# The fifth key tile of each attention block in split form

## Chip, cores and metric

The kernel runs on one core of a Trainium2 chip. The metric is the time of one execution on the device in microseconds (us). Engines are named as TensorE (PE in the profile, its weight loads PEld), VectorE (DVE), ScalarE (ACT), GpSimd (POOL) and SyncE (SP).

## The reference

A trunk of two layers over 1024 latent tokens and 256 context tokens, width 1024. The first layer (gMLP and S5 mixers) is not touched by the change. The second is grouped-query attention: 8 query heads of 128, 2 key/value heads, so 4 query heads share one key/value head. Queries and keys are normalised and rotated, and every latent query sees all 1280 keys:

```python
def _attend(q, k, v):
    s = jnp.einsum('btkgd,bskd->bkgts', q, k).astype(jnp.float32) * (HEAD_DIM ** -0.5)
    p = jax.nn.softmax(s, axis=-1).astype(v.dtype)
    return jnp.einsum('bkgts,bskd->btkgd', p, v)

# in _odd_layer, per block of 128 queries:
    o = lax.map(lambda qi: _attend(qi, k_all, v), qb)
    x = x + gt * ((o_lat * jax.nn.silu(gate[:, n_ctx:])) @ w_out)
```

All values are float32. A final RMSNorm follows.

## The kernel before

The attention stage is a loop over 16 blocks `i` (8 groups of 128 queries x 2 key/value heads). A block holds 4 heads x 128 queries = 512 columns. Its 1280 keys are `TT` = 10 tiles `t` of 128. All engines run over the same running number `m = 10 i + t`, each with its own program, and semaphores tie them together.

**Split form.** A float32 product is made of rounded high parts and low parts (the rest after rounding, in the fp32r type): high x high, high x low and low x high, three matmuls. For the values this is `Vh`/`Vl` and `p_hi`/`p_lo`. Tiles listed in `plain` are multiplied natively instead: one float32 instruction on `Vt` and `PF`, which the trace shows as two MATMUL records.

**Per tile.** TensorE makes the scores (`scores`, lines 2189 to 2191, for t < 2 with one more matmul that subtracts the row maximum, line 2186). ScalarE takes the exp into `PF[m % 5]` (line 1101) and, unless the tile is plain, rounds it into `p_hi` (line 1104, recorded as line 737). The low part `p_lo = PF - p_hi` is made on GpSimd for the tiles in `on_pool` (1 and 6, line 714) and on VectorE for the other split tiles (line 1681), one step of the loop later. GpSimd also adds up `PF` over the tiles in `psum_p` (line 710). TensorE multiplies with the values (`values`) four tiles later (`LAG` = 4): line 2206 for plain tiles, lines 2208 to 2210 for split ones. `PF[4]` and `PF[3]` lie in `region_b`, the others in `region_c`.

**Per block, besides.** TensorE makes the maxima's scores of the next block (`max_scores`, line 2161) at t = 0, 2, 4, 6, one head each; VectorE reduces them (`row_max`, line 1627) at the same t; at t = 8 TensorE transposes the four maxima (`max_rows`) and VectorE turns them into `neg_max` (line 1633), which the first scores of the next block read. The sums of the block before come by `row_sums` on TensorE at t = 4 (line 2219), `sums_copy` on ScalarE, `sums_to_tokens` on TensorE at t = 5, the reciprocal on VectorE (`sums_inverse`, t = 5, line 1647), four transposes `over_sums` on TensorE at t = 6 (recorded as line 1742), and `gate_over_sums` and `output` on VectorE at t = 7. Rounding of the next queries and their low part (`q_rest`, line 1622) come at t = 9.

**Order.** Each engine works in program order. TensorE at a step t of block i: `values(m - 4)`, `scores(i, t)`, then `row_sums`, `sums_to_tokens` or `over_sums` (t = 4, 5, 6), then `max_scores` or `max_rows`. VectorE at a step: `p_lo` of the tile before, then `row_max`, then `sums_inverse`, `gate_over_sums` and `output`, `neg_max` or `q_rest`. These two lines of `values` and VectorE's loop are the ones on which the change acts:

```python
                if t in plain:
                    mm = te.matmul(o, Vt[:, t, hd], PF[m % NP], start=t == 0, stop=t == TT - 1)
...
                if m and (m - 1) % TT not in on_pool + plain:
                    dve.wait_ge(*p_done(m - 1))
```

**V's split.** At the start of the loop ScalarE and VectorE split V in four pieces, per key/value head and half. `split_tiles(half)` gives the tiles of a half that are not plain: 0 to 3 and 5 to 8.

Of the kernel before, what the change touches and what calls it, by code (L numbers as in the profile page):

```python
# [61 lines left out]
def build(nc, x, ctx_in, xt_in, cols_in, w_mod, we_in, we_out, gm_w_s, gm_b_s,  # L62
          lam_in, s5_log_dt, b_in, c_in, s5_d, s5_w_glu, wo_in, wo_out, q_norm_g, k_norm_g, final_g,
          ident_in, cos_in, sin_in, out):
    with ExitStack() as es:
# [311 lines left out]
        def x1_done(t):  # L377
            return s_o_ok, TT + t + 1

        plain, on_pool = (4, 9), (1, 6)  # L380

        def upto(tiles, m):
            return len(tiles) * (m // TT) + sum(t <= m % TT for t in tiles)
# [1984 lines left out]
```

## Time and profile before

| | us |
|---|---|
| median of 3 runs | 1199.05 (1198.66 to 1199.93) |
| the profiled execution | 1199.77 |
| its span on the core | 1198.0 |
| TensorE busy | 1150.5 (96%) |
| VectorE busy | 826.9 (69%) |
| ScalarE busy | 501.8 (42%) |
| GpSimd busy | 427.4 (36%) |

The attention loop runs from about 801 to about 1107 us. In a timeline row the first number is the start in us from the span's beginning, the second the duration; then engine, line, operation, output and inputs, shapes and count. A number in brackets at the end is the idle time of the engine ahead of that instruction and who ended it. Records of one engine can overlap by some hundredths, since an instruction starts while the one before is still writing.

### The profile page before, as it was taken

The page shows a single profiled execution, that of the slowest core. Times are in us where ns is not written, and L with a number is a line of the kernel's source. Part 1 is how long each engine was busy: PE and PEld are TensorE (multiplying, and loading weights), DVE is VectorE, ACT ScalarE, POOL GpSimd, SP SyncE. Part 2 cuts the span into 40 slices and gives each one's busy share as a digit, 9 for nine tenths or more (in the row PEclk, how much of TensorE's full clock was granted, in tenths as well). Part 3 has the DMA queues.
Part 4 walks back from the last instruction along what each step waited for, and adds up shares of the span by engine and source line. Part 5 has one row for each costly group of instructions (what it writes and reads, how often), then busy time and mean ns, then how long its engine had stood idle before and what let it go on. Part 6 is the DMA issues. An engine that isn't in the chain of part 4 may idle for free.

```text
span 1198.0 us, 16737 instructions
## 1 busy us (share of the span) xinstructions
PE 1150.5 (96%) x6498; PEld 943.5 (79%) x6498; DVE 826.9 (69%) x1264; ACT 501.8 (42%) x948; POOL 427.4 (36%) x336
## 2 busy tenths in 40 slices
PE   2899999999999999999999999999999999999996
PEld 2678889887888987878888888876777777777885
DVE  5599959899916365037839968249888888884237
ACT  3444567110014642134523442246666666664022
POOL 4810100000000002542211112248898888897232
PEclk9899999999999999999999999999999999999999
DMA  9933896435421946213121122230000000000403
GB/s 339 369 115 114 197 283 221 142 112 176 156 90 55 323 148 233 71 41 134 38 71 36 36 80 79 88 124 9 10 18 10 18 19 10 18 10 27 165 21 130
DMA packets 81023, 129.83 MB, mean 108 GB/s; under 512 B 12944, under 2 KB 43024, under 8 KB 80144
## 3 DMA queue, kind: packets, MB, share of 16 engines
q1 hardware_dynamic: 71120, 113.96, 28.2%
q10 hardware_dynamic: 9824, 14.80, 3.5%
q8 instruction: 52, 0.85, 0.3%
q14 instruction: 27, 0.22, 0.1%
HBM read 97.81 MB, written 30.93 MB: 107 GB/s over the span
## 4 chain that ended last, share of the span: by engine, by line
PE 88%; DVE 6%; DMA 3%; ACT 1%; issue 1%; POOL 1%; SPq 0%; DVEq 0%; ACTq 0%
PE ps L1877 10%; PE ps L1879 10%; PE ps L1878 10%; PE ps L1888 6%; PE ps L1889 6%; PE ps L1890 6%; PE ps L2161 3%; PE ps L1742 3%; DMA weight_ring<-in_w_mod 3%; PE ps L2191 3%; PE ps L2190 3%; PE ps L2189 3%; PE ps L2245 2%; PE ps L2247 2%; PE ps L2246 2%; PE ps L2208 2%
## 5 line engine op out<-in xcount | busy, mean ns | idle before, releaser
L1877 PE MATMUL ps<-w_hi,a_hi 128*128 128x512 f32 x448 | 177.6, 397 | 4.7 <-DVE b_lo L1221 3.3
L1878 PE MATMUL ps<-w_lo,a_hi 128*128 128x512 f32 x448 | 175.4, 392 | 0.0
L688 POOL TENSOR_TENSOR region_b<-region_b,region_d 128x512 f32<-128x512 f32 x20 | 26.3, 1328 | 397.0 <-DVE region_d L1533 397.0
L1879 PE MATMUL ps<-w_hi,c_lo 128*128 128x512 f32 x368 | 143.3, 389 | 0.0
L1888 PE MATMUL ps<-a_hi,w_hi 128*128 128x512 f32 (+1 forms) x384 | 137.9, 359 | 0.0
L1889 PE MATMUL ps<-b_lo,w_hi 128*128 128x512 f32 (+1 forms) x384 | 136.0, 354 | 0.0
L1890 PE MATMUL ps<-a_hi,w_lo 128*128 128x512 f32 (+1 forms) x384 | 135.9, 354 | 0.0
L681 POOL TENSOR_TENSOR w_lo<-weight_ring,w_hi 128x2048 fp32r<-128x2048 f32 x14 | 65.1, 4652 | 185.5 <-ACT w_hi L737 185.5
L1627 DVE TENSOR_REDUCE small<-ps 128x1 f32<-128x1280 f32 x64 | 95.2, 1487 | 41.7 <-PE ps L2161 41.4
L710 POOL TENSOR_TENSOR region_c<-region_c 128x512 f32<-128x512 f32 x80 | 108.5, 1356 | 26.2 <-ACT region_c L1101 25.1
L1877 PEld LDWEIGHTS ps<-w_hi,a_hi 128*128 128x128 f32 x448 | 84.8, 189 | 24.4 <-issue 5.1
L710 POOL TENSOR_TENSOR region_c<-region_c,region_b 128x512 f32<-128x512 f32 x64 | 98.7, 1542 | 9.2
L1878 PEld LDWEIGHTS ps<-w_lo,a_hi 128*128 128x128 f32 x448 | 84.9, 189 | 17.2
L1101 ACT ACTIVATE region_c<-ps 128x512 f32<-128x512 f32 x96 | 57.3, 597 | 77.2 <-PE ps L2191 74.6
L1681 DVE TENSOR_TENSOR p_lo<-region_c,p_hi 128x512 fp32r<-128x512 f32 x64 | 81.5, 1273 | 11.7 <-ACT p_hi L737 11.7
L737 ACT ACTIVATE w_hi<-weight_ring 128x2048 fp32r<-128x2048 f32 x29 | 55.6, 1916 | 71.3 <-DMA weight_ring<-in_we_out 30.3
L1888 PEld LDWEIGHTS ps<-a_hi,w_hi 128*128 128x128 f32 x384 | 72.5, 189 | 11.4 <-issue 1.1
L1890 PEld LDWEIGHTS ps<-a_hi,w_lo 128*128 128x128 f32 x384 | 72.5, 189 | 10.2
L1879 PEld LDWEIGHTS ps<-w_hi,c_lo 128*128 128x128 f32 x368 | 69.1, 188 | 14.4
L1889 PEld LDWEIGHTS ps<-b_lo,w_hi 128*128 128x128 f32 x384 | 72.6, 189 | 9.6
L737 ACT ACTIVATE region_d<-ps 128x512 f32<-128x512 f32 (+5 forms) x90 | 49.1, 605 | 34.8 <-DMA bop_scratch<-region_d 13.9
L2189 PE MATMUL ps<-q_t_hi,kd_hi 128*128 128x512 f32 x128 | 62.9, 492 | 0.7 <-ACT region_c L1101 0.5
(253 smaller groups left out, 2679.1 us busy)
## 6 DMA issues: line engine op xcount, KB each, us to landing
weight_ring<-in_w_mod SPq DMA_DIRECT2D x10, 2048.0 KB, 9.1
weight_ring<-in_we_in SPq DMA_DIRECT2D x10, 1024.0 KB, 6.8
weight_ring<-in_wo_in SPq DMA_DIRECT2D x10, 1024.0 KB, 5.1
weight_ring<-cop_t_scratch SPq DMA_DIRECT2D x4, 1536.0 KB, 7.7
region_c<-in_w_mod SPq DMA_DIRECT2D x2, 2048.0 KB, 20.0
bop_scratch<-region_d ACTq DMA_DIRECT2D x16, 256.0 KB, 2.9
cop_t_scratch<-region_d SPq DMA_DIRECT2D x8, 512.0 KB, 7.2
weight_ring<-bop_scratch SPq DMA_DIRECT2D x2, 2048.0 KB, 11.3
```

The costliest lines, as they stand in the source:

```text
L681: g.tensor_tensor(wl, slot_raw(u), wh.bitcast(F32), ALU.subtract).then_inc(s_w_lo, 1)
L710: g.tensor_tensor(psum_p[:, i % 2], PF[(m - 1) % NP] if t == 1 else psum_p[:, i % 2], PF[m % NP], ALU.add).then_inc(s_a_sum, 1)
L737: return a.activation(o, i, ACT.Copy)
L1627: v.tensor_reduce(smax[:, i % 2, h:h + 1], ps[:, 0:3, :].rearrange("p b n -> p (b n)")[:, 0:TOK], AX.X, ALU.max).then_inc(s_a_max, 1)
L1681: v.tensor_tensor(p_lo[:, (m - 1) % NP], PF[(m - 1) % NP], p_hi[:, (m - 1) % NP].bitcast(F32), ALU.subtract).then_inc(s_a_pld, 1)
L1877: te.matmul(o, th, wh[:, k % 4], start=k == 0, stop=False)
L1878: te.matmul(o, th, wl[:, k % 4], start=False, stop=False)
L1879: last = te.matmul(o, tl, wh[:, k % 4], start=False, stop=k == KT - 1)
L1888: te.matmul(o, wh[:, k, fs], th, start=k == 0, stop=False)
L1889: te.matmul(o, wh[:, k, fs], tl, start=False, stop=False)
L1890: last = te.matmul(o, wl[:, k, fs], th, start=False, stop=k == KT - 1)
L2189: te.matmul(o, kh, qh, start=False, stop=False, skip_group_check=t >= 2)
```

## The change

Tile 4 leaves the list of plain tiles; tile 9 stays in it.

```diff
-        plain, on_pool = (4, 9), (1, 6)
+        plain, on_pool = (9,), (1, 6)
```

What follows from it in each of the 16 blocks: TensorE multiplies tile 4 with three split matmuls (lines 2208 to 2210) instead of the native one (line 2206), and waits ahead of them for its low part instead of for its exp; ScalarE rounds tile 4 into `p_hi` after its exp; VectorE makes `p_lo` of tile 4 at step t = 5, behind the row maximum of t = 4 and ahead of `sums_inverse`. ScalarE's exp of tile 9 also waits for the rounding and the low part of tile 4, whose buffer it takes. `split_tiles(0)` becomes 0 to 4, so that the two pieces of V of the first half grow from 512 to 640 columns on ScalarE and on VectorE; the counts of `p_done`, `p_rest_done` follow. GpSimd's work is the same.

## Rows read from the trace of the kernel before

**Rows 1.** Table by stretches: one block; busy per engine, granted clock, DMA share, GB/s
```profile
951.10:969.67 18.57, 18.57 (x92) 14.17 (x90) 15.93 (x16) 12.10 (x22) 16.29 (x12) 1.00 0.04 15
```

**Rows 2.** Timeline of TensorE: the slots of tile 3 and tile 4
```profile
945.51 0.39 PE L2208 MATMUL ps<-p_hi,v_hi 128*128 128x512 f32 x1
...
946.67 0.40 PE L2191 MATMUL ps<-q_t_hi,k_t_lo 128*128 128x512 f32 x1
946.90 1.02 PE L2206 MATMUL ps<-region_b 128*128 128x512 f32 x2
...
948.23 0.40 PE L2191 MATMUL ps<-q_t_hi,k_t_lo 128*128 128x512 f32 x1
```

**Rows 3.** Timeline of VectorE, the next block
```profile
954.19 0.68 DVE L1681 TENSOR_TENSOR p_lo<-region_c,p_hi 128x512 fp32r<-128x512 f32 x1
...
961.01 1.48 DVE L1627 TENSOR_REDUCE small<-ps 128x1 f32<-128x1280 f32 x1
962.41 0.17 DVE L1647 RECIPROCAL small<-ps 128x4 f32<-128x4 f32 x1
963.05 1.21 DVE L1681 TENSOR_TENSOR p_lo<-region_c,p_hi 128x512 fp32r<-128x512 f32 x1 [0.47 <-ACT p_hi L737]
...
968.38 0.67 DVE L1633 SCALAR_TENSOR_TENSOR neg_max<-ps,ident 4x512 fp32r<-4x512 f32 x1
```

**Rows 4.** Timeline of ScalarE, the same block
```profile
959.73 0.27 ACT L737 ACTIVATE mod_row<-ps 128x128 f32<-128x128 f32 x1
...
962.38 0.63 ACT L737 ACTIVATE p_hi<-region_c 128x512 fp32r<-128x512 f32 x1
```

**Rows 5.** Timeline of TensorE, the same block: around `over_sums`, and its end
```profile
962.83 0.59 PEld L1742 LDWEIGHTS ps<-ident,small 128*128 128x128 f32 x4
963.07 0.60 PE L1742 MATMUL ps<-ident,small 128*128 128x128 f32 x4
963.42 0.83 PE L2161 MATMUL ps<-k_t_hi,q_t_hi 128*128 128x512 f32 x3
...
969.67 0.39 PE L2186 MATMUL ps<-neg_max,ones_r 128*128 128x512 f32 x1
```

**Rows 6.** Timeline of GpSimd: the sum of tile 5 in the same block
```profile
962.43 1.28 POOL L710 TENSOR_TENSOR region_c<-region_c 128x512 f32<-128x512 f32 x1 [0.20 <-ACT region_c L1101]
```

**Rows 7.** Timeline of VectorE and GpSimd at two near ties ahead of the loop
```profile
590.88 0.43 DVE L1133 TENSOR_TENSOR region_b<-region_b,rec_tmp 128x256 f32<-128x256 f32 x1
590.91 4.86 POOL L681 TENSOR_TENSOR w_lo<-weight_ring,w_hi 128x2048 fp32r<-128x2048 f32 x1 [19.41 <-ACT w_hi L737]
...
664.62 4.61 POOL L681 TENSOR_TENSOR w_lo<-weight_ring,w_hi 128x2048 fp32r<-128x2048 f32 x1 [14.11 <-ACT w_hi L737]
664.65 4.86 DVE L1133 TENSOR_TENSOR region_d<-region_d 128x256 f32<-128x256 f32 x1
```

**Rows 8.** Timeline of VectorE and TensorE behind the loop: a reciprocal that is waited for
```profile
1111.77 0.18 DVE L1647 RECIPROCAL small<-ps 128x4 f32<-128x4 f32 x1 [14.64 <-PE ps L1742]
1112.01 0.65 PE L1742 MATMUL ps<-ident,small 128*128 128x128 f32 x4 [0.28 <-DVE small L1647]
1112.42 0.48 PE L1877 MATMUL ps<-w_hi,ot_hi_a 128*128 128x512 f32 x1
```

**Rows 9.** Timeline of block 0: GpSimd, VectorE and TensorE
```profile
813.45 1.29 POOL L710 TENSOR_TENSOR region_c<-region_c 128x512 f32<-128x512 f32 x1
813.51 1.78 DVE L1681 TENSOR_TENSOR p_lo<-region_c,p_hi 128x512 fp32r<-128x512 f32 x1
...
820.62 0.47 PE L2186 MATMUL ps<-neg_max,ones_r 128*128 128x512 f32 x1 [0.54 <-issue]
```

**Rows 10.** Timeline of block 1: GpSimd (two records in one row), VectorE and TensorE
```profile
832.48 2.99 POOL L710 TENSOR_TENSOR region_c<-region_c 128x512 f32<-128x512 f32 x2
832.51 0.17 DVE L1647 RECIPROCAL small<-ps 128x4 f32<-128x4 f32 x1
833.03 0.60 PE L1742 MATMUL ps<-ident,small 128*128 128x128 f32 x4
```

## The prediction

> **What bounds the kernel now.** I read the table by stretches first, for one attention block out of the middle of the loop [rows 1]: in 18.57 us TensorE is busy for all 18.57, at a granted clock of 1.00 (its 2.4 GHz level), VectorE for 15.93, GpSimd for 16.29 and ScalarE for 12.10. There are 16 such blocks. So a block lasts as long as its TensorE instructions, and whatever makes TensorE wait is lost. VectorE has 2.6 us of air in a block, but where the air lies decides. The timeline by engine shows that: VectorE has no idle time (a number in brackets) ahead of the third row maximum and of the reciprocal behind it, and 0.47 us after that [rows 3]. The reciprocal is what TensorE needs next.
>
> **TensorE, the gain.** With tile 4 out of `plain`, its two native records become three split matmuls. In the slot of tile 4 the native form takes from 946.90 to the last score matmul at 948.23, 1.33 us; the same slot of tile 3 in split form from 945.51 to 946.67, 1.16 us [rows 2]. Both hold two of the three score matmuls besides, so the difference is the edit's: 0.17 us a block. The slot lies in blocks 0 to 15, but in block 0 TensorE waits for VectorE anyway, so 15 x 0.17 = 2.6 us is the most that the change can give. The Trainium skill (FP8 and Floating Point Precision, section TensorE Precision Notes) says that true FP32 takes four passes through the array. By that rule three passes save a quarter, and where the rows give 0.17 us the page would give somewhat more, about 0.2 us; the sum below would fall by some 0.6 us, and its sign would stay.
>
> **ScalarE, nothing.** It gets one rounding copy a block, `p_hi` of tile 4, 0.63 us like that of tile 5 [rows 4]. Behind it is queued the copy of the sums, which runs from 959.73 to 960.00 and would end by 960.67. TensorE fetches the sums one tile ahead of the transposes of 963.07 [rows 5]: less 1.16 us for the tile and 0.35 us for itself that is 961.56, so 0.9 us of cover are left. If it were gone, each 0.1 us would be 0.1 us on TensorE.
>
> **VectorE, the price.** It gets one subtraction a block, `p_lo` of tile 4, and the loop puts it at t = 5 ahead of `sums_inverse`. The queue there is: row maximum at 961.01, reciprocal at 962.41 to 962.58, idle 0.47, `p_lo` of tile 5 at 963.05 [rows 3]. Its data are ready by about 960.5, so it would start where the reciprocal starts today. Queued behind it are the reciprocal and, for that, TensorE's four transposes of `over_sums`, whose weight load begins at 962.83 and whose first matmul at 963.07, with the row-max matmuls of the next head at 963.42 [rows 5]. The idle 0.47 us comes after the reciprocal and so is no cover for it; the cover is 0.25 us, from 962.58 to 962.83.
>
> How long the subtraction takes depends on GpSimd. With GpSimd idle it took 0.68 us (954.19), and 1.21 and 1.78 us when GpSimd ran a tensor operation [rows 3, 9]. The rows show how: `p_lo` at 963.05 ends at 964.26, 0.55 us after GpSimd's operation of 962.43 ends at 963.71 [rows 3, 6]; that of 813.51 ends at 815.29, 0.55 us after the operation of 813.45 ends at 814.74 [rows 9]. So with two inputs from SBUF the one that comes second waits until the other is through. At the place of the new subtraction both come together: VectorE would start at 962.41, GpSimd's sum of tile 5 at 962.43 [rows 3, 6]. Near ties elsewhere tell who goes first [rows 7]: at 590.88 VectorE starts 0.03 us ahead, keeps its 0.43 us, and GpSimd's operation is stretched to 4.86 from the 4.61 us of its twin at 664.62; at 664.65, 0.03 us behind GpSimd, VectorE is held for 4.86 us. Here VectorE is ahead by 0.02 us and goes first, I estimate. Both ends: 0.61 us to the next start (0.68 less the 0.07 by which these records overlap) if it wins, 1.77 us if it loses (962.43 + 1.28 + 0.55, less the overlap, against 962.41). I take 0.61, the nearest rows in distance.
>
> Then the reciprocal starts at 963.02 and ends at 963.19. In the last block TensorE really waits for one: it ends at 1111.95, the transposes start 0.06 us later and the next matmul 0.41 us after that [rows 8], against 0.35 us when nothing waits [rows 5]. So the row-max matmul comes at 963.19 + 0.06 + 0.41 = 963.66 and not 963.42: a loss of 0.24 us, less 0.17 gained, net +0.07 us.
>
> Is another wait then last? GpSimd is pushed back by 0.53 us in its sum of tile 5, `p_lo` of tile 5 now waits for it and ends near 964.79, the fourth row maximum starts at 964.71 and `neg_max` at about 968.90 instead of 968.38 [rows 3]. It ends at 969.57; TensorE needs it for the first matmul of the next block at 969.67 today, 969.74 then [rows 5]. It fits, by about 0.1 us. Bounds for a steady block: -0.05 (half the loss) to +0.30 us (that margin gone too).
>
> **Block 0.** Here VectorE is late and TensorE waits for it, at the end of the block 0.54 us for `neg_max`, until 820.62 [rows 9]. All added here is paid in full. At its place (813.51) GpSimd starts 0.06 us ahead, so the subtraction takes what `p_lo` of tile 5 takes there now, 1.78 us, 1.71 from start to start. `split_tiles(0)` now spans five tiles, so two ScalarE copies and two VectorE subtractions of V have 640 instead of 512 columns: 0.13 us more each on VectorE (1280 columns took 1.40 us from start to start, 512 take 0.61 [rows 3]), two of them before `neg_max`. Together 1.71 + 0.26 = 1.97 us; bounds 0.9 and 2.3.
>
> **Block 1.** GpSimd's start is 0.03 us ahead of VectorE's reciprocal at 832.51 [rows 10], so the subtraction waits: 832.48 + 1.28 (GpSimd's 962.43 row) + 0.55 gives 834.31, reciprocal to 834.41, transposes at 834.47 against 833.03 [rows 10]. 1.44 + 0.06 - 0.17 = +1.33 us; bounds 0 and 1.4.
>
> **Last block.** No row maxima are there; the new subtraction ends close to the reciprocal's old place: about 0.1 us lost, 0.17 gained, -0.1 us. Behind the loop nothing changes.
>
> **Sum.** 1.97 + 1.33 + 13 x 0.07 - 0.1 = +4.1 us. The profiled execution took 1199.77 us, 1198.0 of it the span; it would be 1203.9. It lies 0.7 us above the median of 1199.05, so the median becomes 1203.1. With the bounds: 0.9 + 0 - 0.7 - 0.1 = +0.1 to 2.3 + 1.4 + 3.9 - 0.1 = +7.5 us.
>
> **Rivals.** (1) GpSimd wins the tie in every block. Then the subtraction ends at 964.26, the reciprocal at 964.35, the row-max matmul comes at 964.82: 1.40 lost, 0.17 gained, 13 x 1.23 = 16.0, total +19.2 us, 1218.2 us. It decides from a GpSimd start 0.01 to 0.03 us earlier against VectorE. For it speaks that the distance is tiny and that a subtraction behind a row maximum lost at 0.06 us [rows 9]; against it stand the near ties [rows 7]. The Trainium skill (GPSIMD Engine Reference, section Key points) says that GpSimd shares its SBUF interfaces with VectorE and contends with instructions of two SBUF inputs; by that rule alone this case is the plain one, and the trace agrees that they contend, though not that VectorE always pays. (2) Faster: TensorE does not wait at `over_sums`, since the reciprocal is out by 962.77 after all. The deciding point is 0.4 us: VectorE would have to reach this place by that much earlier. Then 15 x 0.17 = 2.6 us come off, 1196.5 us if block 0 costs nothing. Against it: no idle VectorE time ahead of the third maximum and the reciprocal [rows 3]. (3) The steady blocks come out even and block 0 or 1 absorbs part: +0.5 to +2 us, about 1200.5. For it: the bounds of the small terms.
>
> **How the numbers follow.** Forecast 0.72 (its own spread 1200.5 to 1206.6, since the small terms will hardly all lie at the same end), rival 1 with mixtures 0.12, rival 2 0.06, rival 3 0.10. The range 1199.6 to 1207.5 leaves out rival 1 and rival 2 and a little of rival 3. A measurement of this kernel tells 0.2%, 2.4 us, from no change. Faster by that needs rival 2 nearly whole: 0.05. Within it: rival 3, the low end of the forecast (below 1201.4) and the rest of rival 2: 0.18. Slower: 0.77.
>
> **What would show it.** Steady blocks of about 18.64 us; the reciprocal 0.6 us later behind the third row maximum, with `p_lo` of tile 4 of 0.68 us between; GpSimd's sum of tile 5 stretched to about 1.8 us; TensorE idle some 0.2 us before the transposes of `over_sums`. If that subtraction reads 1.8 us, rival 1 holds; if TensorE has no idle time there, rival 2. Wrong also if `neg_max` ends last at a block's border, or if block 0 grows by less than 1 us.

## The result, and the profile after

| us | before | after |
|---|---|---|
| median of 6 runs of each | 1198.88 (1197.69 to 1199.93) | 1203.43 (1202.88 to 1203.74) |
| the profiled execution | 1199.77 | 1203.29 |
| its span | 1198.0 | 1201.5 |

The ratio of after to before is 1.0033, interval 1.0024 to 1.0043: slower, by 4.6 us in the medians and by 3.5 us in the two profiled spans. The forecast was 1203.1, made of +4.1 us on the span and the place of the profiled execution of before among its runs. On the span +4.1 is 0.6 us too high; that the median comes within 0.3 us is in part chance.

The attention loop was measured block by block, from the first row-max matmul of a block (line 2186) to that of the next:

| block | before | after | difference | forecast |
|---|---|---|---|---|
| 0 | 19.82 | 21.80 | +1.98 | +1.97 |
| 1 | 19.02 | 18.72 | -0.30 | +1.33 |
| 2 | 18.59 | 18.66 | +0.07 | +0.07 |
| 3 to 13, each | 18.573 | 18.683 (18.65 to 18.72) | +0.110 | +0.07 |
| 14 | 18.14 | 18.64 | +0.50 | +0.07 |
| last, and all behind it | 117.29 | 117.29 | -0.01 | -0.1 |

With the stretch ahead of the loop (+0.07) that is 1.98 - 0.30 + 0.07 + 11 x 0.110 + 0.50 - 0.01 + 0.07 = +3.5 us. The forecast was near because its errors cancel: one term, block 1, is 1.6 us too high, and the others are 1.0 us too low together. That is luck.

The first line of the page of after (busy time, share, instructions) answers to the table of before: VectorE has 18.6 us more, about 13 of it the 16 new subtractions (14 of 0.68 us; those of block 0 and the last block are held by GpSimd and take 1.78) and the rest mostly other operations held longer behind GpSimd; ScalarE has 10 us more; TensorE is as long as it was, 1150.8 us against 1150.5, since records last longer while they wait: in the middle block below they cover 18.70 of 18.71 us.

```profile
PE 1150.8 (96%) x6514; PEld 943.4 (79%) x6514; DVE 845.5 (70%) x1280; ACT 512.1 (43%) x964; POOL 435.6 (36%) x336
```

The table by stretches of after, block 0 and a block out of the middle (length; busy time of TensorE, its weight loads, VectorE, ScalarE, GpSimd; granted clock; DMA share, GB/s), answers to [rows 1]:

```profile
800.87:822.67 21.80, 16.84 (x71) 11.83 (x70) 19.55 (x15) 15.75 (x26) 17.15 (x12) 1.00 0.26 85
953.45:972.16 18.71, 18.70 (x93) 14.21 (x92) 17.08 (x17) 12.73 (x23) 16.86 (x13) 1.00 0.06 16
```

In block 0 TensorE stands still for 5 us, VectorE for 2.3. In the middle block TensorE seems never to stand still. That is a trap: a matmul's record lasts some 0.4 us, while the next one starts 0.23 us after it when nothing waits. A wait under 0.17 us hides inside a record, and only the distance from start to start shows it.

The timeline of VectorE in that block of after, from the third row maximum to `neg_max`, answers to [rows 3]:

```profile
963.46 1.48 DVE L1627 TENSOR_REDUCE small<-ps 128x1 f32<-128x1280 f32 x1
964.86 0.68 DVE L1681 TENSOR_TENSOR p_lo<-region_b,p_hi 128x512 fp32r<-128x512 f32 x1
965.45 0.17 DVE L1647 RECIPROCAL small<-ps 128x4 f32<-128x4 f32 x1
965.55 1.67 DVE L1681 TENSOR_TENSOR p_lo<-region_c,p_hi 128x512 fp32r<-128x512 f32 x1
...
969.92 1.53 DVE L1681 TENSOR_TENSOR p_lo<-region_c,p_hi 128x512 fp32r<-128x512 f32 x1
971.38 0.67 DVE L1633 SCALAR_TENSOR_TENSOR neg_max<-ps,ident 4x512 fp32r<-4x512 f32 x1
```

The timeline of GpSimd, same stretch, answers to [rows 6]:

```profile
964.88 1.79 POOL L710 TENSOR_TENSOR region_c<-region_c 128x512 f32<-128x512 f32 x1 [0.20 <-ACT region_c L1101]
967.10 1.29 POOL L710 TENSOR_TENSOR region_c<-region_c 128x512 f32<-128x512 f32 x1 [0.43 <-POOL region_c L710]
968.35 1.30 POOL L714 TENSOR_TENSOR p_lo<-region_c,p_hi 128x512 fp32r<-128x512 f32 x1
969.60 1.30 POOL L710 TENSOR_TENSOR region_c<-region_c 128x512 f32<-128x512 f32 x1
```

VectorE starts the new subtraction at 964.86, GpSimd its sum of tile 5 at 964.88. VectorE goes first and takes 0.68 us; GpSimd waits inside its record, 1.79 instead of 1.28 us. It is so in blocks 1 and 3 to 14; in block 2 GpSimd starts 0.25 us behind, and the order is the same. And the timeline of TensorE, at `over_sums` and at the block's end, answers to [rows 5]:

```profile
965.27 0.40 PE L2191 MATMUL ps<-q_t_hi,k_t_lo 128*128 128x512 f32 x1
965.68 0.65 PE L1742 MATMUL ps<-ident,small 128*128 128x128 f32 x4
966.09 0.71 PE L2161 MATMUL ps<-k_t_hi,q_t_hi 128*128 128x512 f32 x2
...
971.92 0.40 PE L2210 MATMUL ps<-p_hi,v_lo 128*128 128x512 f32 x1
972.16 0.46 PE L2186 MATMUL ps<-neg_max,ones_r 128*128 128x512 f32 x1
972.46 0.40 PE L2189 MATMUL ps<-q_t_hi,k_t_hi 128*128 128x512 f32 x1
```

The transposes come 0.06 us after the reciprocal's end (965.62), 0.41 instead of 0.23 us behind the matmul before, and the next matmul 0.41 instead of 0.35 us behind them: 0.24 us, as forecast. But the border costs too. `neg_max` ends at 972.05, its matmul starts 0.11 us later, and the one behind that 0.30 instead of 0.23 us later, because its weights weren't loaded ahead: another 0.07 us. (At 8 of the 15 borders the matmul starts 0.101 to 0.102 us after `neg_max`, the least in this run, so it waits itself.) TensorE's weight load for the matmul at this border, in after and then in before, where it begins 0.24 us ahead of its matmul of 969.67 and not 0.04 us:

```profile
972.12 0.19 PEld L2186 LDWEIGHTS ps<-neg_max,ones_r 128*128 128x128 f32 x1 [0.23 <-issue]
...
969.43 0.19 PEld L2186 LDWEIGHTS ps<-neg_max,ones_r 128*128 128x128 f32 x1
```

The waits of TensorE's weight loads, from 820 to 1080 us of after (total, times, longest), show the two places (for the second the profile names no engine; experiment 5 shows that it is `neg_max`); in before the first is missing and the second has one wait:

```profile
PEld ps L1742 <- DVE small L1647: 6.2, 14, 0.4
...
PEld ps L2186 <- issue: 4.5, 14, 1.5
```

### The profile page after: what moved, and what is told of

It reads as the page before. It is cut to its first block, busy times and chain, and to the rows that moved or that the text cites. A ratio compares the mean times of both kernels' runs of the same rounds, so it can differ in the third digit from the quotient of the medians.

```text
span 1201.5 us, 16817 instructions
## 1 busy us (share of the span) xinstructions
PE 1150.8 (96%) x6514; PEld 943.4 (79%) x6514; DVE 845.5 (70%) x1280; ACT 512.1 (43%) x964; POOL 435.6 (36%) x336
## 4 chain that ended last, share of the span: by engine, by line
PE 86%; DVE 6%; DMA 3%; POOL 2%; issue 1%; ACT 1%; SPq 0%; POOLq 0%; DVEq 0%; ACTq 0%
PE ps L1877 10%; PE ps L1879 10%; PE ps L1878 10%; PE ps L1888 6%; PE ps L1890 6%; PE ps L1889 6%; PE ps L1742 3%; PE ps L2161 3%; DMA weight_ring<-in_w_mod 3%; PE ps L2189 3%; PE ps L2190 3%; PE ps L2191 3%; PE ps L2208 2%; PE ps L2210 2%; PE ps L2247 2%; PE ps L2246 2%
## 5 line engine op out<-in xcount | busy, mean ns | idle before, releaser
L710 POOL TENSOR_TENSOR region_c<-region_c 128x512 f32<-128x512 f32 x80 | 116.0, 1450 | 21.9 <-ACT region_c L1101 19.0
L1681 DVE TENSOR_TENSOR p_lo<-region_c,p_hi 128x512 fp32r<-128x512 f32 x64 | 90.4, 1412 | 4.0 <-ACT p_hi L737 4.0
L2191 PE MATMUL ps<-q_t_hi,k_t_lo 128*128 128x512 f32 x160 | 62.7, 392 | 0.0
```

The lines of the kernel that those rows point to most:

```text
L710: g.tensor_tensor(psum_p[:, i % 2], PF[(m - 1) % NP] if t == 1 else psum_p[:, i % 2], PF[m % NP], ALU.add).then_inc(s_a_sum, 1)
L1681: v.tensor_tensor(p_lo[:, (m - 1) % NP], PF[(m - 1) % NP], p_hi[:, (m - 1) % NP].bitcast(F32), ALU.subtract).then_inc(s_a_pld, 1)
L2191: te.matmul(o, kl, qh, start=False, stop=True, skip_group_check=t >= 2).then_inc(s_a_s, 1)
```

## The experiments

Unless said otherwise, the edit is made to the changed kernel. "Steady" is the length of blocks 3 to 13. Times are medians; the kernel before was measured again beside the experiments, and its medians there, 1199.7 to 1200.0, lie about 1 us above the one of the table. So an experiment is compared with after by blocks or by the profiled spans, 1201.5 us for after and 1198.0 for before.

**1. Without the subtraction.** Tile 4 is multiplied in three parts, but its high part stands in for the low one. The counts of `p_rest_done` follow.

```diff
-                if m and (m - 1) % TT not in on_pool + plain:
+                if m and (m - 1) % TT not in on_pool + plain + (4,):
...
-                    te.matmul(o, Vh[:, t, hd], p_lo[:, m % NP], start=False, stop=False)
+                    te.matmul(o, Vh[:, t, hd], p_hi[:, m % NP] if t == 4 else p_lo[:, m % NP], start=False, stop=False)
```

> The changed kernel without VectorE's subtraction for tile 4. What is left out: the low part of tile 4's exp; TensorE multiplies p_hi of tile 4 twice instead of p_hi and p_lo. ScalarE's rounding and the larger V pieces stay. Theory: the price is VectorE's subtraction alone. Then a steady block, border to border, is 18.57 - 0.17 = 18.40 us, block 0 is 19.82 + 0.26 = 20.1 us, and the span is 2.0 to 2.5 us below that of the kernel before. Rival (the split matmuls or ScalarE's copy cost as much as they bring): a steady block stays at 18.57 to 18.68 us and the span is not below the kernel before.

1196.45 us against 1199.96 (ratio 0.9972, interval 0.9961 to 0.9983). Steady 18.380, block 0 20.14. So TensorE gains 18.573 - 18.380 = 0.193 us a block by the split form, and the rest of after is VectorE's subtraction: 18.683 - 18.380 = 0.303 us a steady block, 1.66 us in block 0. The remaining 0.3 us of block 0 is put down to V's wider pieces, which this kernel keeps; no run took them away alone. The profiled span is 1195.4 us, 2.6 below before (expected 2.0 to 2.5); the 3.5 us in the medians are more than the blocks account for.

**2. The reciprocal first.** If the reciprocal is what TensorE lacks, it could go ahead of the new subtraction.

```diff
+                if i and t == 5:
+                    sums_inverse(i - 1)
                 if m and (m - 1) % TT not in on_pool + plain:
...
-                if i and t == 5:
-                    sums_inverse(i - 1)
```

> The changed kernel with one order turned round: VectorE computes the reciprocal of the sums first and subtracts tile 4 behind it. Theory (the share of SBUF with GpSimd decides): the subtraction then starts about 0.1 us later, 0.08 us behind GpSimd's sum of tile 5 and no longer 0.02 us ahead of it, and is held for about 1.75 us; the wait at over_sums is gone, but row maximum and neg_max come 1 to 1.5 us later and end last at the block's border: a steady block of 19.5 to 20.0 us, the span 12 to 20 us above the changed kernel. Rival (only the place of the reciprocal in VectorE's order costs): the wait at over_sums is gone and nothing takes its place, a steady block of 18.40 to 18.50 us, the span 2.5 to 3.5 us below the changed kernel.

1220.10 us (ratio 1.0169, interval 1.0153 to 1.0186), steady 20.03. The transposes no longer wait, and the span is 16 us longer than that of after (1217.5 against 1201.5). VectorE's timeline, then GpSimd's:

```profile
971.51 0.17 DVE L1647 RECIPROCAL small<-ps 128x4 f32<-128x4 f32 x1
971.60 1.75 DVE L1683 TENSOR_TENSOR p_lo<-region_b,p_hi 128x512 fp32r<-128x512 f32 x1
973.27 1.79 DVE L1683 TENSOR_TENSOR p_lo<-region_c,p_hi 128x512 fp32r<-128x512 f32 x1
...
971.51 1.28 POOL L710 TENSOR_TENSOR region_c<-region_c 128x512 f32<-128x512 f32 x1 [0.18 <-ACT region_c L1101]
```

The reciprocal's 0.09 us are enough for GpSimd to be first. (In block 2, where GpSimd comes later, VectorE stays first and the block takes 18.77 us.) The subtraction is held until 0.55 us after GpSimd's sum, and the next one behind another operation of GpSimd. TensorE pays later, for a row maximum and for `neg_max`:

```profile
976.52 0.27 PE L1742 MATMUL ps<-ident,small 128*4 128x128 f32 x1 [0.43 <-DVE small L1627]
...
980.14 0.47 PE L2186 MATMUL ps<-neg_max,ones_r 128*128 128x512 f32 x1 [0.82 <-issue]
```

**3. Losing the tie.** A copy of one column goes ahead of the subtraction on VectorE, nothing else.

```diff
+                if m % TT == 5:
+                    v.tensor_copy(small[:, 334:335], small[:, 0:1])
```

> The changed kernel with one tiny VectorE copy of one column (about 0.07 us from start to start) ahead of the subtraction of tile 4 in each block. Theory: it turns the near tie round, GpSimd goes first, the subtraction reads about 1.75 instead of 0.68 us, the reciprocal comes 1.1 to 1.2 us later, and a steady block grows from 18.68 to 19.8 us: 15 to 17 us in all for 16 tiny instructions. Rival (the subtraction's length has nothing to do with who starts first): the block grows by the 0.07 us of the copy, 1 us in all.

1216.48 us in one run, steady 19.76 to 19.82. VectorE, GpSimd and TensorE:

```profile
970.85 0.14 DVE L1680 COPY small<-small 128x1 f32<-128x1 f32 x1
970.91 1.78 DVE L1683 TENSOR_TENSOR p_lo<-region_b,p_hi 128x512 fp32r<-128x512 f32 x1
972.62 0.17 DVE L1647 RECIPROCAL small<-ps 128x4 f32<-128x4 f32 x1
...
970.87 1.28 POOL L710 TENSOR_TENSOR region_c<-region_c 128x512 f32<-128x512 f32 x1 [0.20 <-ACT region_c L1101]
...
972.84 0.65 PE L1744 MATMUL ps<-ident,small 128*128 128x128 f32 x4 [1.18 <-DVE small L1647]
```

The copy moves the subtraction by 0.06 us, from 0.02 us ahead of GpSimd to 0.04 behind. That costs 1.1 us a block, and TensorE's wait is now plain to see. Block 2 is the check within the run: GpSimd starts a quarter of a microsecond later there, VectorE stays first in spite of the copy, and the block takes 18.65 us.

**4. The subtraction on GpSimd.** GpSimd has the lowest share of busy time on the page, 36%.

```diff
-        plain, on_pool = (9,), (1, 6)
+        plain, on_pool = (9,), (1, 4, 6)
```

> The changed kernel with the subtraction of tile 4 on GpSimd (on_pool = (1, 4, 6)). Theory: VectorE's queue ahead of the reciprocal is as in the kernel before, GpSimd has 2.3 us of air in a block and takes 1.28 more, so a steady block is 18.40 us, block 0 within 0.5 us of the kernel before, and the span 1.5 to 2.5 us below the kernel before. Rival (GpSimd becomes the bound, or holds VectorE longer): GpSimd's air is not where it is needed, row_sums or neg_max wait for it, a steady block of 18.6 us or more.

1216.42 us (ratio 1.0136, interval 1.0120 to 1.0151), steady 19.65. My theory missed by 1.2 us a block. The 36% are an average over the whole span; inside the loop GpSimd has no such room. The table by stretches, 40 us of the loop, and TensorE waiting for it:

```profile
960.00:1000.00 40.00, 38.45 (x187) 29.16 (x186) 34.43 (x31) 25.78 (x45) 38.42 (x28) 1.00 0.05 14
...
976.79 0.50 PE L2208 MATMUL ps<-p_hi,v_hi 128*128 128x512 f32 x1 [0.77 <-POOL p_lo L714]
```

GpSimd is busy for 38.42 of 40 us and is now what the block lasts on: its operations take 1.72 to 1.75 us where VectorE's turn comes first.

**5. `neg_max` earlier.** In the last step of a block `neg_max` goes ahead of VectorE's subtraction of tile 7 (the step's `p_lo`), which is held by GpSimd.

```diff
+                if i + 1 < 2 * LT and t == 8:
+                    neg_max(i + 1)
                 if m and (m - 1) % TT not in on_pool + plain:
...
-                if i + 1 < 2 * LT and t == 8:
-                    neg_max(i + 1)
```

> The changed kernel with neg_max ahead of the subtraction of tile 7 on VectorE (t = 8), all else as it is. Theory: of a steady block's 18.68 us, about 0.06 us are TensorE's wait for neg_max at the border and the rest of the loss against 18.38 us is the wait at over_sums. neg_max then starts 1.4 us earlier, the border wait goes, the wait at over_sums stays: a steady block of 18.62 us, the block ahead of the last 18.2 instead of 18.64 us; blocks 0 and 1 together 0.5 to 1 us shorter, the span 1.5 to 2.5 us below the changed kernel. Rival (the border wait costs nothing, the loss of 0.30 us is all at over_sums): steady blocks stay at 18.68 us.

1200.03 us against 1199.73 of before (ratio 1.0006, interval 0.9997 to 1.0015). Blocks 3 to 13 are 18.61, block 14 is 18.16, blocks 0 and 1 together 0.99 us shorter than in after, the span 2.7 us shorter. So the border's wait was real, and it was nearly all that block 14 had lost. The wait for the reciprocal stays: 18.61 - 18.38 = 0.23 us.

**6. Block 0 as before.** Tile 4 stays native in block 0 alone. V's tile 4 is then split by itself, later in block 1.

```diff
+        def is_plain(m):
+            return m % TT in plain or m == 4
...
+                if m == 16:
+                    dve.wait_ge(s_v_hi, 5)
+                    dve.wait_ge(s_a_pv, 1)
+                    v.tensor_tensor(Vl[:, 4], Vt[:, 4], Vh[:, 4].bitcast(F32), ALU.subtract).then_inc(s_v_lo, 1)
```

> The changed kernel with tile 4 native in block 0 alone; V's tile 4 is split by itself in block 1. Theory: block 0 falls from 21.80 to 19.8 us as in the kernel before. Block 1 then begins as in the kernel before, where GpSimd's sum started 0.03 us ahead of VectorE, so the subtraction of tile 4 is held there, as the prediction had it: block 1 of 20.2 to 20.5 us, the span 0.2 to 0.6 us below the changed kernel. Rival (VectorE is first in block 1 in any case): block 1 of 18.7 to 19.1 us, the span about 2 us below the changed kernel.

1204.09 us in one run: block 0 is 19.83 again, and block 1 becomes 21.31, where 20.2 to 20.5 were expected. Nothing is saved: the span is 0.8 us above that of after. This is the experiment on the forecast's block 1, which was worked out as if block 0 ended as before; here it does. VectorE, GpSimd and TensorE in block 1:

```profile
832.86 1.79 DVE L1689 TENSOR_TENSOR p_lo<-region_b,p_hi 128x512 fp32r<-128x512 f32 x1
...
832.83 1.28 POOL L716 TENSOR_TENSOR region_c<-region_c 128x512 f32<-128x512 f32 x1
...
834.80 0.65 PE L1754 MATMUL ps<-ident,small 128*128 128x128 f32 x4 [1.25 <-DVE small L1655]
...
838.22 0.47 PE L2222 MATMUL ps<-p_hi,v_hi 128*128 128x512 f32 x1 [0.78 <-DVE v_lo L1700]
```

GpSimd is 0.03 us ahead and the subtraction takes 1.79 us, as forecast. V's extra piece, which this edit brings in and the expectation had at nothing, costs more than the idle 0.78 us: the matmul of 838.22 starts 1.18 us behind the one of 837.04 instead of 0.23, and the next one 0.30 us behind it instead of 0.23, 1.02 us in all. The other wait, at `over_sums`, counts in the same way (1.65 instead of 0.24 us ahead of the transposes and 0.41 instead of 0.35 behind them, less the gain of 0.19) for +1.28 us. The two add up to the 2.3 us by which block 1 is longer than before, and +1.33 was forecast for the second.

**7. GpSimd told to wait.** Experiment 2, with the sum of tile 5 on GpSimd held until the subtraction of tile 4 is done.

```diff
+                    if t == 5:
+                        pool.wait_ge(*p_rest_done(m - 1))
```

> The changed kernel with the reciprocal first on VectorE, as in b_recip_first, and GpSimd's sum of tile 5 waiting until the subtraction of tile 4 is done. Theory: the order costs nothing once the turn on SBUF is fixed; the subtraction reads 0.68 us, neither over_sums nor neg_max is waited for, a steady block of 18.38 us as without the subtraction; block 0 of 20.7 to 21.3 us since it stays VectorE's; the span 1.0 to 2.0 us below the kernel before. Rival (GpSimd's chain of sums or VectorE's queue is late by the wait): a steady block of 18.5 us or more.

1204.41 us (ratio 1.0039, interval 1.0025 to 1.0052), where 1.0 to 2.0 us below before were expected: the rival held. Block 0 is 20.00, better than expected, since VectorE now goes first there too. Blocks 1 and 2 are 18.42 and 18.50, then it gives way to 18.82 to 19.15. GpSimd held for the subtraction and TensorE waiting for GpSimd, in block 8; then VectorE's subtraction ahead of `neg_max` and TensorE at the border, in block 5:

```profile
965.19 1.63 POOL L712 TENSOR_TENSOR region_c<-region_c 128x512 f32<-128x512 f32 x1 [0.68 <-DVE p_lo L1685]
...
970.29 0.50 PE L2210 MATMUL ps<-p_hi,v_hi 128*128 128x512 f32 x1 [0.41 <-POOL p_lo L716]
...
911.87 1.70 DVE L1685 TENSOR_TENSOR p_lo<-region_c,p_hi 128x512 fp32r<-128x512 f32 x1
...
914.27 0.47 PE L2188 MATMUL ps<-neg_max,ones_r 128*128 128x512 f32 x1 [0.20 <-issue]
```

The order costs GpSimd 0.68 us of idle time a block. Its later operations come later, the subtraction of tile 7 is held behind one of them for 1.70 us, and `neg_max` starts 17.22, 17.73 and 18.07 us after the border in blocks 1, 2 and 3. From block 2 on TensorE waits for it at the end of every block but block 8. There VectorE comes first instead (0.72 us), and TensorE waits for the low part that GpSimd makes; at 19.15 us it is the longest of these blocks.

**8. Experiments 6 and 7 together.**

> g_pool_after and f_block0_native together. Theory: block 0 as in the kernel before (19.8 us), steady blocks 18.38 us, the span 2.3 to 3.0 us below the kernel before, a ratio of 0.9975 to 0.998. Rival: what block 0 saves comes back in block 1 (over 19.4 us), and the span is no lower than that of g_pool_after.

1204.79 us (ratio 1.0042, interval 1.0030 to 1.0055). The rival held again: block 0 is 19.84, but block 1 is 20.37, with the wait for V's extra piece. Blocks 2 and 3 are 18.40 and 18.38, then 18.71, 18.83 and on as in 7, so the waits at the border begin in block 4 instead of block 2.

**9. The transposes later.** On TensorE, `over_sums` goes behind the row-max matmuls of the same step.

```diff
-                if i and t == 6:
-                    over_sums(i - 1)
                 if i + 1 < 2 * LT:
...
+                if i and t == 6:
+                    over_sums(i - 1)
```

> The changed kernel with TensorE's four transposes over_sums behind the row-max matmuls of t = 6 instead of ahead of them, 0.57 us later. Theory: the wait at over_sums goes, since the reciprocal is done by then, but neg_max ends when it did, so TensorE only meets it earlier at the block's border: a steady block of 18.60 to 18.66 us with 0.2 to 0.3 us of waiting at neg_max, the span 0.3 to 1.0 us below the changed kernel. Rival (the wait at over_sums is the whole loss): a steady block of 18.38 to 18.42 us, the span some 3.5 us below the changed kernel.

1203.50 us against 1199.95 (ratio 1.0027, interval 1.0018 to 1.0037), steady 18.70, neither the 18.60 to 18.66 of the theory nor the rival's 18.38. The waits of TensorE's weight loads from 820 to 1080 us show the other one alone, and grown:

```profile
PEld ps L2186 <- issue: 8.1, 14, 1.6
```

The wait for the reciprocal is gone, and nothing is won: `neg_max` by itself costs 0.32 us a block. The near tie is as near as the trace can show here: in block 5 both engines start at 906.97, VectorE 0.003 us ahead, and VectorE takes 0.68 us, GpSimd 1.82.

**10. Both orders together (5 and 9).**

> The changed kernel with both orders changed: over_sums behind the row-max matmuls of t = 6, and neg_max ahead of the subtraction of tile 7. Theory: both waits for VectorE go, the near tie stays won, and a steady block is that without the subtraction, 18.38 to 18.42 us; the span 1.5 to 2.5 us below the kernel before, a ratio of 0.9980 to 0.9990. Rival (a third wait takes their place, in VectorE's or GpSimd's queue): a steady block of 18.5 us or more and a span not below the kernel before.

1198.86 us against 1199.95 (ratio 0.9989, interval 0.9980 to 0.9998): 1.1 us under before (1.5 to 2.5 expected) and, by the spans, 4.4 us under after. The 1.1 us are a difference whose interval ends just short of 1 and that is smaller than what this kernel's measurement can tell from no change. Blocks 4 to 13 take 18.353 each, block 14 17.91. VectorE and TensorE at the two places:

```profile
962.26 1.49 DVE L1683 TENSOR_TENSOR p_lo<-region_b,p_hi 128x512 fp32r<-128x512 f32 x1
963.68 0.17 DVE L1647 RECIPROCAL small<-ps 128x4 f32<-128x4 f32 x1
...
968.15 0.67 DVE L1633 SCALAR_TENSOR_TENSOR neg_max<-ps,ident 4x512 fp32r<-4x512 f32 x1
...
963.55 0.73 PE L2161 MATMUL ps<-k_t_hi,q_t_hi 128*128 128x512 f32 x3
964.12 0.60 PE L1742 MATMUL ps<-ident,small 128*128 128x128 f32 x4
...
969.94 0.39 PE L2186 MATMUL ps<-neg_max,ones_r 128*128 128x512 f32 x1
970.17 0.40 PE L2189 MATMUL ps<-q_t_hi,k_t_hi 128*128 128x512 f32 x1
```

The subtraction takes 1.49 us here, held by GpSimd's sum of tile 4, and nothing waits: the transposes start 0.27 us after the reciprocal's end, and `neg_max` ends 1.12 us before its matmul. So the near tie did not stay won, as the theory had it; VectorE comes to this place 0.7 us earlier in the block than in after, and the later transposes cover what it loses. Block 3 is the one that took 19.25 us. VectorE, then GpSimd, there:

```profile
870.33 1.81 DVE L1683 TENSOR_TENSOR p_lo<-region_b,p_hi 128x512 fp32r<-128x512 f32 x1
...
870.31 1.29 POOL L710 TENSOR_TENSOR region_c<-region_c 128x512 f32<-128x512 f32 x1
```

GpSimd is first by 0.03 us, and TensorE waits for the reciprocal: it is experiment 3 over again, once.

**11. Both orders on the kernel before.** The control for 10: is it the orders alone?

> The kernel before, with the two new orders of j_both alone; tile 4 stays native. Theory: nothing waits for VectorE in its steady blocks, so they stay at 18.57 us; only blocks 0 and 1, where neg_max is late, may get shorter, by up to 1 us in all. Rival (the two orders are worth something by themselves, and j_both's gain is theirs): steady blocks below 18.55 us.

1199.40 us against 1199.95 (ratio 0.9996, interval 0.9987 to 1.0005), steady 18.533: the orders alone give 0.04 us a block. By its own mark (below 18.55) the rival is right about that much, and why is not shown. Blocks 0 and 1 (19.12 and 19.67) are together no more than 0.05 us shorter than before, where up to 1 us was expected. Of the 0.22 us by which a block of 10 is shorter than one of before, 0.18 are then the change's own, if the two add up; the gain of experiment 1 was 0.193.

## Why the prediction was right, and where it was wrong

**What bounds the kernel: right.** A steady block is TensorE's instructions plus what makes it wait.

**TensorE, the gain: mechanism right, size short.** Forecast 0.17 us a block by two slots of the timeline, measured 0.193 by experiment 1. The slot of tile 3 stood for that of tile 4, but in experiment 1 the slot of tile 4 in split form takes 1.145 us, not 1.16, and 15 blocks multiply such an error. The Trainium skill (FP8 and Floating Point Precision, section TensorE Precision Notes) counts four passes for true FP32. By an estimate from that rule three split matmuls save a quarter, about 0.2 us, and the measured 0.193 agrees with it better than my slots did.

**ScalarE, nothing: right.** No wait of TensorE goes back to the copy of the sums or to a rounding, in after or in experiment 10, and experiment 1, which keeps the rounding, has the whole gain.

**VectorE, the price: right, and it is what decided the case.** The subtraction takes 0.68 us with VectorE 0.02 us ahead, GpSimd's sum 1.79 us (forecast about 1.8), `over_sums` loses 0.24 us. That rival 1's price was right as well is shown by experiment 3: 19.76 to 19.82 us a block, forecast 19.8.

**The margin of `neg_max`: wrong.** "It fits, by about 0.1 us" failed, though the numbers beside it even left 0.17 us (969.74 less 969.57). I had `neg_max` 0.52 us later within the block; it is 0.65 later (17.93 us after the border, where 968.38 lay 17.28 behind the border of 951.10 [rows 1, 3]). I let only GpSimd's sum of tile 5 slip. But GpSimd's next sum waits for that one (the 0.43 at 967.10) and all that follows on GpSimd comes 0.6 us later, also its operation of 969.60, behind which the subtraction ahead of `neg_max` takes its turn: 1.53 instead of 1.38 us. And I compared the end of `neg_max` with the start of its matmul as if nothing lay between; 0.10 us do. The 0.17 less 0.13 and 0.10 are 0.06 us short, and that is the wait of 0.07 us in a steady block (0.303 lost where 0.24 were forecast). It is also nearly all of block 14, which is shorter on TensorE and has less cover: +0.50 instead of +0.07, of which experiment 5 takes back 0.48. "Wrong also if `neg_max` ends last at a block's border" was one of my signs, and by it the path of a steady block was wrong in this part. I had held it to the bound of +0.30; blocks 2 to 13 lie inside it, block 14 does not.

**Block 0: right**, 1.98 against 1.97. Of it experiment 1 gives 1.66 to the subtraction and leaves 0.32 for V's pieces, where I had 1.71 and 0.26.

**Block 1: wrong.** Forecast +1.33 us, measured -0.30. I took VectorE's and GpSimd's starts from block 1 of before, where GpSimd is 0.03 us ahead. But this change makes block 0 2 us longer, and with that the two engines come into block 1 at another distance. The timeline of after, VectorE and GpSimd in block 1:

```profile
834.12 0.68 DVE L1681 TENSOR_TENSOR p_lo<-region_b,p_hi 128x512 fp32r<-128x512 f32 x1
834.72 0.17 DVE L1647 RECIPROCAL small<-ps 128x4 f32<-128x4 f32 x1
...
834.14 1.79 POOL L710 TENSOR_TENSOR region_c<-region_c 128x512 f32<-128x512 f32 x1 [0.20 <-ACT region_c L1101]
```

VectorE is 0.02 us ahead, as in a steady block. Experiment 6, with block 0 as it was, brings the held subtraction of 1.79 us back, and with it +1.28 us where +1.33 was forecast. The step that failed is not the price but the starting point: a tie of 0.03 us can't be read from a trace of a program whose previous block will change.

**The rest.** The last block and all behind it are as long as before (-0.01, forecast -0.1). But the path there was not the forecast's: GpSimd is 0.33 us ahead, the new subtraction takes 1.78 us, and the reciprocal ends 1.0 us later; in before it had ended that long ahead of its transposes, so little is lost. And the range of 1199.6 to 1207.5 does not follow from the bounds +0.1 and +7.5 us, which put on the median of 1199.05 give 1199.2 to 1206.6; the result lies inside both.

**What remains open.** Why VectorE is ahead by 0.02 us in nearly every block, and not behind, is not settled. GpSimd's sum follows ScalarE's exp of tile 5 (the 0.20 us in brackets). VectorE comes by its own queue, which has no idle time in the 6 us ahead of its subtraction. The runs show that a hundredth or two of a microsecond decide the case (experiments 3 and 10), not what sets them. Nor is it settled what the new orders give by themselves (0.04 us a block in experiment 11).

## What to carry to other kernels

Where two engines share a resource in turns, look at the distance of their starts, not at their busy time: an operation put in front, even one of 0.06 us, can turn 0.68 us into 1.78 us, and a gain that hangs on such a tie is not safe (block 3 of experiment 10). Two waits of nearly the same size on one engine hide each other; taking away one gives a small part of the gain (5) or none (9), and only both together give all of it. Follow a delay around the loop and through every engine to the next border before calling a margin safe, and don't price a block by a trace whose previous block the change makes longer.

## What the runs showed of the hardware

VectorE and GpSimd, both with two inputs from SBUF, don't slow each other down gradually. They take turns by whole instructions: the second ends 0.54 us after the first (VectorE 972.69, GpSimd 972.15 in experiment 3) or is stretched by 0.5 us (GpSimd, 1.28 to 1.79 us), and the one that starts first, by 0.02 us in after and by 0.003 us in experiment 9, pays nothing. The Trainium skill (SBUF — State Buffer, section SBUF: two separate sides) says that the pair of ports they share is an exclusive lock and that whichever starts first has it for the whole instruction; the runs agree in both directions, 0.68 us for VectorE ahead and 1.78 us for VectorE behind. A weight load that wasn't issued ahead of its matmul cost 0.06 to 0.07 us (start to start 0.30 instead of 0.23 us at the border, 0.41 instead of 0.35 us behind the transposes).
